# An S5/MLA encoder kernel on one core: GpSimd makes each block's powers in halves of four groups

## The chip, the cores and the metric

The kernel runs as one program on one core of a Trainium2 chip. The metric is the device time of one execution in microseconds (us). Before the change three executions took 1778.18, 1778.20 and 1778.39 us, a median of 1778.2 us.

The engines are named as the profile names them: PE is TensorE (PEld its weight loads), DVE is VectorE, ACT is ScalarE, POOL is GpSimd, and SP is SyncE, which here only issues DMAs.

## The reference, cut to what matters

Two layers over 512 positions with 1024 channels. Each layer is a half SwiGLU (1024 to 2816 and back), a mixer, and another half SwiGLU. The mixer of layer 0 is S5, a diagonal complex state-space model in 64 groups of 16 channels with 64 states; that of layer 1 is attention over a shared latent K/V.

```python
step = jnp.exp(log_step)[:, None]
lam_bar = jnp.exp(lam * step)                    # (64 groups, 64 states), complex
b_bar = ((lam_bar - 1.0) / lam)[..., None] * b
bu = einsum('gpc,bsgc->bsgp', b_bar, u)
x_t = lam_bar * x_{t-1} + bu_t                   # associative scan over 512 steps
y = einsum('gcp,bsgp->bsgc', c_re, re(x)) - einsum('gcp,bsgp->bsgc', c_im, im(x)) + d_skip * h
z = gelu(y) @ w_glu;  out = z[..., :1024] * sigmoid(z[..., 1024:])
```

The kernel takes the scan in steps of T = 8 positions. For that it needs, for each group, the powers of lam_bar up to the eighth multiplied into B and into C, and from these products small matrices (taps, and B turned) that the S5 stage uses. The change is in the making of these products.

## The kernel before, in words

The weights come as a stream of 296 packs of 128x1024 floats (N_LOADS), in order of use, into a ring of four buffers. ACT rounds each pack to its high part (split, L765), DVE subtracts to get the low part (split, L1182), and PE does three matmuls for each product of 128x128 weights with 128x512 activations: L1636, L1637 and L1638 in `three`.

The first SwiGLU is cut into two stages of 11 tiles each, FFN0A1 and FFN0A2 (HALF = 11). In the IN part of a stage PE makes a gate and an up tile for each f (48 matmuls), and DVE and ACT turn them into one tile of G: `gated` on DVE is L1192 (gate times rstd), L1194 (silu times up) and L1196 (low part of G, g_split), with ACT's L771 and L773 between them. PE starts tile f + 2 only when L1194 of tile f has read its banks (s_read). In the OUT part PE sums over the 11 tiles for each of 8 output tiles d, and DVE adds them to the residual (L1284, L1285).

The preparation of S5 runs beside these two stages, in 8 blocks of 8 groups (GB = 8, block k holds groups 8k to 8k + 7):

- POOL first makes the tables of powers (L381 to L386 in `cmul`, with 64 to 512 elements a partition), then `make_powers(k)` for each block (L564 to L600), the subject of the change. It starts the load of the next block's B and C (L581), waits for its own, and makes C times the powers in CP (L584, L589, L591, 8x9x16 = 1152 elements a partition) and B times the powers in BP (L594, L595, L597, 8x8x16 = 1024 elements). It waits on its own semaphore s_cp between a product and the subtraction that reads it. The last one raises s_made; then POOL issues the DMA that stores CP (L599). The second product into CP (L589) waits for PE's turn of the block before (s_turned) and for the store of its CP (s_cpst), because CP and BP exist once.
- Blocks 0, 1 and 2 follow each other on POOL, with more of the tables in between. Block 3 waits until the eleventh tile of G is done (L658). From block 4 on each block waits for the turn before it.
- PE turns block k in `turn_block` (L1697 to L1715): it waits for s_made, then does 16 small matmuls (L1709) and 8 transposes (L1713). Where this stands in PE's order is written out by hand in TURN_AT (L83): behind IN tiles 5, 7, 9 and OUT tile 3 of the first stage, and IN tiles 1, 3, 5, 7 of the second. PE works in order: while it waits for s_made it does nothing else.
- ACT copies the turned block out of PSUM (`copy_ops`), DVE adds the skip to the taps (`block_taps`, L1236 and L1239), and DVE makes the tables of phases (`block_tables`, L1225 to L1231: four products of 512 elements with no wait between them, a wait, then two sums). SP stores the results and needs them all before the S5 stage starts. The places in DVE's order are TAPS_AT and TABLES_AT.

```python
TURN_AT = {(FFN0A1, IN, 5): 0, (FFN0A1, IN, 7): 1, (FFN0A1, IN, 9): 2, (FFN0A1, OUT, 3): 3, (FFN0A2, IN, 1): 4,
           (FFN0A2, IN, 3): 5, (FFN0A2, IN, 5): 6, (FFN0A2, IN, 7): 7}
```

On POOL `tt` is `nc.gpsimd.tensor_tensor`. Operations of one engine are issued in order; a wait in the text is a wait of the whole engine.

Of the kernel before, what the change touches and what calls it, by code (L numbers as in the profile page):

```python
# [28 lines left out]
ALU = mybir.AluOpType  # L29
# [15 lines left out]
T = 8  # L45
STEPS = SEQ // T
GB = 8
BLOCKS = GROUPS // GB

M = T + 1  # L50
# [61 lines left out]
def build(nc, xT, wstream, cols, consts, mask, pos, lam, bcd, dskip, out):  # L112
# [40 lines left out]
    def tmp(name, shape, dt=F32):  # L153
        t = at(name, shape, dt, t_at[0])
        t_at[0] += (int(np.prod(shape[1:])) * 4 + 31) // 32 * 32
        assert t_at[0] <= o_w
        return t

    LAM = tmp("lam", [P, 3, GROUPS])
    PW = tmp("lam_pow", [P, 2, M, GROUPS])  # L160
    PWS = tmp("lam_pow_signed", [P, 2, M, GROUPS])
# [4 lines left out]
    CP = tmp("c_pow", [P, GB, M, GC])  # L166
    BP = tmp("b_pow", [P, GB, T, GC])
# [47 lines left out]
    def sem(name):  # L215
        return nc.alloc_semaphore(name)
# [31 lines left out]
    s_cp = sem("c_and_b_steps")  # L248
# [6 lines left out]
    s_made, s_turned, s_taps, s_btc = sem("powers_made"), sem("ops_turned"), sem("taps_ready"), sem("b_op_copied")  # L255
# [31 lines left out]
    def block_groups(k):  # L287

        return slice(k * GB, (k + 1) * GB)
# [132 lines left out]
    with nc.Block() as block:  # L422
# [121 lines left out]
        def _(pool):  # L544
# [8 lines left out]
            tt, ts = nc.gpsimd.tensor_tensor, nc.gpsimd.tensor_scalar  # L553
# [10 lines left out]
            def make_powers(k):  # L564

                first = k == 0

                def chan(ap):
                    return ap.rearrange("p (g c) -> p g c", g=GB)

                def power(tab, ri, n):
                    return (tab[:, ri, 0:n, block_groups(k)].rearrange("p m g -> p g m").unsqueeze(3)
                            .broadcast_to([P, GB, n, GC]))

                def spread(ap, n):
                    return chan(ap).unsqueeze(2).broadcast_to([P, GB, n, GC])

                tmc = TM[:].rearrange("p (g m c) -> p g m c", g=GB, m=M)
                tmb = TM[:, 0:GB * T * GC].rearrange("p (g m c) -> p g m c", g=GB, m=T)
                if k + 1 < BLOCKS:  # L580
                    pool.dma_start(BC[(k + 1) % 2][:], bcd[k + 1]).then_inc(s_bc[(k + 1) % 2], 16)  # L581
                bc = BC[k % 2]
                pool.wait_ge(s_bc[k % 2], 16 * (k // 2 + 1))
                tt(tmc, spread(bc[:, 3, :], M), power(PWS, 1, M), ALU.mult)  # L584
                if not first:

                    pool.wait_ge(s_turned, k)
                    pool.wait_ge(s_cpst, k * 16)
                tt(CP[:], spread(bc[:, 2, :], M), power(PWS, 0, M), ALU.mult).then_inc(s_cp, 1)  # L589
                pool.wait_ge(s_cp, k * 3 + 1)  # L590
                tt(CP[:], CP[:], tmc, ALU.subtract).then_inc(s_cp, 1)  # L591

                pool.wait_ge(s_cp, k * 3 + 2)
                tt(BP[:], spread(bc[:, 0, :], T), power(PW, 0, T), ALU.mult)  # L594
                tt(tmb, spread(bc[:, 1, :], T), power(PW, 1, T), ALU.mult).then_inc(s_cp, 1)  # L595
                pool.wait_ge(s_cp, k * 3 + 3)
                tt(BP[:], BP[:], tmb, ALU.subtract).then_inc(s_made, 1)  # L597
                pool.wait_ge(s_made, k + 1)
                pool.dma_start(ops_dram[k][:, O_C:O_T].rearrange("p (g n) -> p g n", g=GB),  # L599
                               CP[:, :, 1:M, :].rearrange("p g m c -> p g (m c)")).then_inc(s_cpst, 16)  # L600
# [41 lines left out]
            e1, e2 = (TM[:, 512 * q:512 * (q + 1)].rearrange("p (m g) -> p m g", m=T) for q in range(2))  # L642
            cmul(tt, link, PW[:, 0, 0:T, :], PW[:, 1, 0:T, :], PW[:, 0, 0:T, :], PW[:, 1, 0:T, :], ec[0], ec[1], e1, e2)
            make_powers(0)


            u1, u2, u4 = (S6[:, 5, :], S6[:, 4, :]), (S6[:, 9, :], S6[:, 10, :]), (S6[:, 11, :], S6[:, 12, :])
            squared(tt, link, u2, u1, t1, t2)
            squared(tt, link, u4, u2, t1, t2)
            squared(tt, link, (PB[:, 0, 1, :], PB[:, 1, 1, :]), u4, t1, t2)  # L650
            make_powers(1)
            powers(tt, link, PB, 7, t1, t2)
            make_powers(2)
            squared(tt, link, (PA[:, 0, 1, :], PA[:, 1, 1, :]), (PB[:, 0, 4, :], PB[:, 1, 4, :]), t1, t2)
            powers(tt, link, PA, 7, t1, t2)
# [1535 lines left out]
```

## Time and profile before

| | before |
|---|---|
| median of 3 executions | 1778.2 us |
| profiled execution | 1779.0 us |
| span of the profiled execution | 1777.2 us |
| PE busy | 1750.6 us (99%) |
| DVE busy | 933.3 us (53%) |
| ACT busy | 650.5 us (37%) |
| POOL busy | 326.4 us (18%), 276 instructions |
| mean granted clock of PE | 0.997 |

The page of the profile describes one execution; times in the trace count from the start of its span. A timeline lists an engine's instructions with their start and their duration, and in brackets the idle time before one and who ended it. A duration holds the time in which an instruction has been issued and can't run yet, so a long duration of an operation that is short elsewhere is a wait inside it. The granted clock is 1.00 for 2.4 GHz and 0.50 for 1.2 GHz. The two stages beside which S5 is prepared take the first 390 us; POOL makes blocks 0 to 2 from 50 to 122 us, and the last block ends at 281 us.

### The profile page before, as it was taken

Reading aid. Unit: us, or ns where it says so; the run is one execution under the profiler, and the core shown is the slowest. Engines: PE = TensorE matmul, PEld = TensorE weight load, DVE = VectorE, ACT = ScalarE, POOL = GpSimd, SP = SyncE. Lnnn points to the kernel's source line nnn. Section 1 sums busy time; section 2 is a strip of 40 time slices with the busy share of each in tenths; the row PEclk is TensorE's granted clock in tenths of the full one; section 3 lists DMA queues with packets and bytes.
Section 4 is the critical chain, followed back from the end, with each engine's and each line's share of the span. In section 5 each row is a group of like instructions: output and inputs, shape, how many; then the busy total and the mean of one; then the engine's idle time right before and its main releaser. Section 6 shows DMA issues by size and latency. Waiting matters only on the chain.

```text
span 1777.2 us, 22438 instructions
## 1 busy us (share of the span) xinstructions
PE 1750.6 (99%) x8598; PEld 1434.4 (81%) x8598; DVE 933.3 (53%) x1066; ACT 650.5 (37%) x896; POOL 326.4 (18%) x276
## 2 busy tenths in 40 slices
PE   9999999998999999999999999999999999999998
PEld 6888887777888888888888888888777888888887
DVE  7778888638555334433374444333774544433333
ACT  6332233347334333322253333222574443333222
POOL 8997273015013000000100000000200200000000
PEclk9999999999999999999999999999999999999999
DMA  5364555868333333333223332333310332333321
GB/s 199 121 171 131 172 158 171 294 223 269 119 95 97 98 101 94 94 95 97 94 85 111 100 94 94 95 96 101 100 36 9 121 96 94 94 95 97 101 87 48
DMA packets 80788, 206.50 MB, mean 116 GB/s; under 512 B 24048, under 2 KB 34416, under 8 KB 79696
## 3 DMA queue, kind: packets, MB, share of 16 engines
q1 hardware_dynamic: 69664, 189.86, 34.4%
q0 software_dynamic: 2592, 13.51, 2.3%
q10 hardware_dynamic: 8464, 2.20, 0.5%
q8 instruction: 47, 0.77, 0.2%
q14 instruction: 21, 0.17, 0.0%
HBM read 182.46 MB, written 23.07 MB: 116 GB/s over the span
## 4 chain that ended last, share of the span: by engine, by line
PE 89%; DVE 5%; ACT 2%; DMA 2%; issue 1%; SPq 1%; ACTq 0%; DVEq 0%
PE bank L1636 28%; PE bank L1637 28%; PE bank L1638 28%; DVE w_split L1182 1%; DMA s_y<-u_and_y 1%; PE bank L1996 1%; ACT w_split L765 1%; PE bank L1975 1%; PE bank L1809 0%; DMA x_res<-xT 0%; SPq L447 0%; DVE d_eye L1236 0%; PE bank L1988 0%; DMA y_tokens<-s_y 0%; PE bank L1713 0%
## 5 line engine op out<-in xcount | busy, mean ns | idle before, releaser
L1182 DVE TENSOR_TENSOR w_split<-w_raw,w_split 128x1024 fp32r<-128x1024 f32 x296 | 404.1, 1370 | 600.5 <-ACT w_split L765 599.6
L1636 PE MATMUL bank<-h_split,w_split 128*128 128x512 f32 x1504 | 589.8, 392 | 4.4 <-DVE gate L1194 2.7
L1638 PE MATMUL bank<-h_split,w_split 128*128 128x512 f32 x1504 | 586.0, 390 | 0.0
L1637 PE MATMUL bank<-h_split,w_split 128*128 128x512 f32 x1504 | 585.9, 390 | 0.0
L765 ACT ACTIVATE w_split<-w_raw 128x1024 fp32r<-128x1024 f32 x296 | 311.8, 1058 | 599.9 <-PE bank L1638 596.3
L1636 PEld LDWEIGHTS bank<-h_split,w_split 128*128 128x128 f32 x1504 | 282.8, 188 | 66.8 <-DVE gate L1194 3.8
L1637 PEld LDWEIGHTS bank<-h_split,w_split 128*128 128x128 f32 x1504 | 282.7, 188 | 59.4 <-issue 1.4
L1636 PE MATMUL bank<-g_split,w_split 128*128 128x512 f32 (+1 forms) x854 | 328.4, 385 | 1.9 <-DVE g_split L1196 1.5
L1638 PEld LDWEIGHTS bank<-h_split,w_split 128*128 128x128 f32 x1504 | 282.7, 188 | 58.9
L1637 PE MATMUL bank<-g_split,w_split 128*128 128x512 f32 (+1 forms) x854 | 327.6, 384 | 0.0
L1638 PE MATMUL bank<-g_split,w_split 128*128 128x512 f32 (+1 forms) x854 | 327.6, 384 | 0.0
L562 POOL TENSOR_TENSOR sq_sum<-sq_sum,sq 128x512 f32<-128x512 f32 x39 | 51.1, 1311 | 1062.5 <-ACT sq L784 953.4
L1636 PEld LDWEIGHTS bank<-g_split,w_split 128*128 128x128 f32 x854 | 160.5, 188 | 34.9 <-DVE g_split L1196 1.9
L1638 PEld LDWEIGHTS bank<-g_split,w_split 128*128 128x128 f32 x854 | 160.5, 188 | 31.8
L1637 PEld LDWEIGHTS bank<-g_split,w_split 128*128 128x128 f32 x854 | 160.5, 188 | 31.2
L771 ACT ACTIVATE gate<-gate 128x512 f32<-128x512 f32 x88 | 55.7, 632 | 232.8 <-DVE gate L1192 232.8
L1196 DVE TENSOR_TENSOR g_split<-gate,g_split 128x512 f32 (+1 forms) x88 | 77.6, 882 | 80.8 <-ACT g_split L773 80.8
L1194 DVE TENSOR_TENSOR gate<-gate,bank 128x512 f32<-128x512 f32 x88 | 60.5, 687 | 62.7 <-ACT gate L771 62.7
L773 ACT ACTIVATE g_split<-gate 128x512 f32 (+1 forms) x88 | 55.6, 632 | 72.7 <-DVE gate L1194 72.7
L1192 DVE TENSOR_TENSOR gate<-bank,rstd 128x512 f32<-128x512 f32 x88 | 60.1, 682 | 1.4 <-ACT rstd L802 1.4
L777 ACT ACTIVATE h_split<-x_res,cols 128x512 fp32r<-128x512 f32 x48 | 33.1, 717 | 52.1 <-DVE x_res L1285 48.2
L784 ACT ACTIVATE sq<-x_res 128x512 f32<-128x512 f32 x41 | 25.6, 624 | 57.3 <-DVE x_res L1285 44.9
(298 smaller groups left out, 1157.1 us busy)
## 6 DMA issues: line engine op xcount, KB each, us to landing
w_raw<-wstream SPq DMA_DIRECT2D x296, 512.0 KB, 3.5
op_slot<-s_ops SPq DMA_DIRECT2D x5, 2048.0 KB, 10.8
s_ops<-ops_out SPq DMA_DIRECT2D x16, 512.0 KB, 3.1
op_slot<-s_ops POOLq DMA_DIRECT2D x3, 2048.0 KB, 14.6
s_ops<-c_pow POOLq DMA_DIRECT2D x8, 512.0 KB, 5.4
s_ops<-k_window SPq DMA_DIRECT2D x64, 64.0 KB, 3.3
x_res<-xT SPq DMA_DIRECT2D x8, 256.0 KB, 6.5
s_u<-x_gained ACTq DMA_DIRECT2D x8, 256.0 KB, 6.1
```

The lines of the kernel that those rows point to most:

```text
L562: nc.gpsimd.tensor_tensor(ACC[:], ACC[:], SQ[:, k % 2, :], ALU.add).then_inc(s_sum, 1)
L765: nc.scalar.activation(W[:, r, 0, :], RAW[:, r, :], ACT.Copy).then_inc(s_hi, 1)
L771: nc.scalar.activation(GT[:], GT[:], ACT.Silu).then_inc(s_silu, 1)
L773: nc.scalar.activation(gt_part(f, 0), GT[:], ACT.Copy).then_inc(s_g_hi, 1)
L777: nc.scalar.activation(dst[:, k, 0, :], X[:, k, :], ACT.Identity, scale=col(gains + k)).then_inc(s_h_hi, 1)
L1182: tt(W[:, r, 1, :], RAW[:, r, :], W[:, r, 0, :].bitcast(F32), ALU.subtract).then_inc(s_lo, 1)
L1192: tt(GT[:], gb[:], RSTD[:], ALU.mult).then_inc(s_gate, 1)
L1194: tt(GT[:], GT[:], ub[:], ALU.mult).then_inc(s_read, 1)
L1196: tt(gt_part(f, 1), GT[:], gt_part(f, 0).bitcast(F32), ALU.subtract).then_inc(s_g_lo, 1)
L1636: mm(bank, hi, x_hi, start=start, stop=True, skip_group_check=True)
L1637: mm(bank, hi, x_lo, start=False, stop=True, skip_group_check=True)
L1638: return mm(bank, lo, x_hi, start=False, stop=True, skip_group_check=True)
```

## The change

Each of the six operations in `make_powers` is issued as two, one for groups 0 to 3 of the block and one for groups 4 to 7, right behind each other. The semaphore is raised by the second. The waits, the order of the six steps, the buffers and the DMAs stay as they are. A block has twelve operations in place of six, and the eight blocks 96 in place of 48.

```diff
+                def in_halves(dst, a, b, op):
+
+                    for gs in (slice(0, GB // 2), slice(GB // 2, GB)):
+                        ins = tt(dst[:, gs], a[:, gs], b[:, gs], op)
+                    return ins
+
...
-                tt(tmc, spread(bc[:, 3, :], M), power(PWS, 1, M), ALU.mult)
+                in_halves(tmc, spread(bc[:, 3, :], M), power(PWS, 1, M), ALU.mult)
                 if not first:
 
                     pool.wait_ge(s_turned, k)
                     pool.wait_ge(s_cpst, k * 16)
-                tt(CP[:], spread(bc[:, 2, :], M), power(PWS, 0, M), ALU.mult).then_inc(s_cp, 1)
+                in_halves(CP, spread(bc[:, 2, :], M), power(PWS, 0, M), ALU.mult).then_inc(s_cp, 1)
                 pool.wait_ge(s_cp, k * 3 + 1)
-                tt(CP[:], CP[:], tmc, ALU.subtract).then_inc(s_cp, 1)
+                in_halves(CP, CP, tmc, ALU.subtract).then_inc(s_cp, 1)
 
                 pool.wait_ge(s_cp, k * 3 + 2)
-                tt(BP[:], spread(bc[:, 0, :], T), power(PW, 0, T), ALU.mult)
-                tt(tmb, spread(bc[:, 1, :], T), power(PW, 1, T), ALU.mult).then_inc(s_cp, 1)
+                in_halves(BP, spread(bc[:, 0, :], T), power(PW, 0, T), ALU.mult)
+                in_halves(tmb, spread(bc[:, 1, :], T), power(PW, 1, T), ALU.mult).then_inc(s_cp, 1)
                 pool.wait_ge(s_cp, k * 3 + 3)
-                tt(BP[:], BP[:], tmb, ALU.subtract).then_inc(s_made, 1)
+                in_halves(BP, BP, tmb, ALU.subtract).then_inc(s_made, 1)
```

## Rows read from the trace of the kernel before

**Rows 1.** The page, busy time of each engine with its share of the span.
```profile
PE 1750.6 (99%) x8598; PEld 1434.4 (81%) x8598; DVE 933.3 (53%) x1066; ACT 650.5 (37%) x896; POOL 326.4 (18%) x276
```

**Rows 2.** Waits of PE, 20 to 420 us: total us, times, longest us.
```profile
PE bank L1636 <- DVE gate L1194: 2.7, 2, 1.9
```

**Rows 3.** Timeline of PE: start us, us; turns of blocks 1, 2, 6, and two waits.
```profile
99.90 0.63 PE L1709 MATMUL bank<-c_pow,b_pow 128*16 128x128 f32 x16
...
123.28 0.63 PE L1709 MATMUL bank<-c_pow,b_pow 128*16 128x128 f32 x16
...
265.74 0.63 PE L1709 MATMUL bank<-c_pow,b_pow 128*16 128x128 f32 x16
...
269.30 0.55 PE L1636 MATMUL bank<-h_split,w_split 128*128 128x512 f32 x1 [1.91 <-DVE gate L1194]
...
336.59 0.50 PE L1636 MATMUL bank<-g_split,w_split 128*128 128x512 f32 x1 [1.50 <-DVE g_split L1196]
```

**Rows 4.** Busy us of PE, PEld, DVE, ACT, POOL; granted clock, DMA share, GB/s.
```profile
269.60:273.00 3.40, 3.40 (x9) 2.65 (x8) 3.06 (x2) 2.21 (x3) 3.24 (x3) 0.50 0.51 187
...
336.00:338.00 2.00, 1.41 (x6) 1.19 (x7) 1.75 (x3) 0.76 (x1) 0.00 (x0) 1.00 1.00 412
```

**Rows 5.** DVE's weight splits, 50 to 136 us and 185 to 219 us.
```profile
L1182 DVE TENSOR_TENSOR w_split<-w_raw,w_split 128x1024 fp32r<-128x1024 f32 x16 | 34.0, 2140 | 8.3 <-ACT w_split L765 7.9
...
L1182 DVE TENSOR_TENSOR w_split<-w_raw,w_split 128x1024 fp32r<-128x1024 f32 x8 | 9.6, 1220 | 4.6 <-ACT w_split L765 4.5
```

**Rows 6.** Timeline of POOL: blocks 1, 2, 5, 6 and 7.
```profile
78.87 2.27 POOL L589 TENSOR_TENSOR c_pow<-bc_in_odd,lam_pow_signed 128x1152 f32<-128x1152 f32 x1
81.21 3.55 POOL L591 TENSOR_TENSOR c_pow<-c_pow,s_tmp 128x1152 f32<-128x1152 f32 x1
...
86.84 2.49 POOL L595 TENSOR_TENSOR s_tmp<-bc_in_odd,lam_pow 128x1024 f32<-128x1024 f32 x1
...
92.96 0.95 POOL L599 DMA_DIRECT2D s_ops<-c_pow  x1 [0.30 <-POOL b_pow L597]
...
121.84 0.95 POOL L599 DMA_DIRECT2D s_ops<-c_pow  x1 [0.30 <-POOL b_pow L597]
...
229.08 2.04 POOL L595 TENSOR_TENSOR s_tmp<-bc_in_odd,lam_pow 128x1024 f32<-128x1024 f32 x1
...
258.41 0.95 POOL L599 DMA_DIRECT2D s_ops<-c_pow  x1 [0.30 <-POOL b_pow L597]
...
269.80 2.65 POOL L591 TENSOR_TENSOR c_pow<-c_pow,s_tmp 128x1152 f32<-128x1152 f32 x1
```

**Rows 7.** Timeline of DVE beside blocks 1, 2, 5, 6 and 7.
```profile
77.78 4.45 DVE L1182 TENSOR_TENSOR w_split<-w_raw,w_split 128x1024 fp32r<-128x1024 f32 x1 [3.70 <-ACT w_split L765]
...
84.92 2.52 DVE L1196 TENSOR_TENSOR g_split<-gate,g_split 128x512 fp32r<-128x512 f32 x1 [0.70 <-ACT g_split L773]
...
93.05 1.21 DVE L1182 TENSOR_TENSOR w_split<-w_raw,w_split 128x1024 fp32r<-128x1024 f32 x1
...
121.96 0.82 DVE L1196 TENSOR_TENSOR g_split<-gate,g_split 128x512 fp32r<-128x512 f32 x1 [0.70 <-ACT g_split L773]
122.91 3.07 DVE L1182 TENSOR_TENSOR w_split<-w_raw,w_split 128x1024 fp32r<-128x1024 f32 x2
...
247.61 0.68 DVE L1192 TENSOR_TENSOR gate<-bank,rstd 128x512 f32<-128x512 f32 x1
...
258.50 1.11 DVE L1225 TENSOR_TENSOR gate<-u_pow 128x512 f32<-128x512 f32 x1
...
262.75 2.65 DVE L1230 TENSOR_TENSOR ops_out<-ops_out,gate 128x512 f32<-128x512 f32 x1
...
267.18 0.68 DVE L1192 TENSOR_TENSOR gate<-bank,rstd 128x512 f32<-128x512 f32 x1
```

**Rows 8.** Timeline of POOL: small operations of the tables, undisturbed.
```profile
26.53 0.32 POOL L386 TENSOR_TENSOR lam_pow<-lam_pow,s_tmp 128x64 f32<-128x64 f32 x1
...
33.33 0.74 POOL L385 TENSOR_TENSOR lam_pow<-lam_pow,s_tmp 128x256 f32<-128x256 f32 x1
```

## Prediction, made before the change was run

> **What bounds the kernel now.** I read the page of the profile first: TensorE (PE) is busy for 99% of the span [rows 1], so the time changes only where PE waits or loses its clock. The waits of PE up to 420 us, around the part that is changed, show two on DVE's gate operations, 2.7 us in all [rows 2]. PE's own timeline then places everything [rows 3]. The turn of block 1 begins at 99.90 and that of block 2 at 123.28: 23.38 us for 96 matmuls and a turn of 1.6 us, 0.227 us a matmul, which is PE's full pace. PE keeps it until 267.4. There it waits 1.91 us for DVE's gate (269.30); two smaller waits follow, 0.78 (the rest of the 2.7) and 1.50 us at 336.59.
>
> The first wait costs more than itself: behind it the granted clock is 0.50 (1.2 GHz, against 1.00 at 2.4 GHz) for 3.4 us, in which 9 matmuls lie where full pace has 15; half of the 3.4, 1.7 us, is lost; behind the wait of 1.50 us the clock stayed at 1.00 [rows 4]. So this part holds 1.9 + 1.7 + 0.8 + 1.5 = 5.9 us that a quicker DVE could give back, and no more.
>
> Why DVE is late there: a weight split (L1182) takes 1.22 us where POOL is idle (185 to 219), and 2.14 us on average while POOL makes powers [rows 5]. The two timelines beside each other show the cause. The split of 77.78 takes 4.45 us and ends at 82.23, right behind POOL's L589 (81.14); L591, issued at 81.21, takes 3.55 us where the one of 269.80 takes 2.65 [rows 6, 7]. A DVE operation with two SBUF inputs and a POOL operation don't run together: each waits for the whole of the other. DVE can get in between two POOL operations with no wait between them: g_split of 84.92, issued during L594, ends at 87.44, 0.6 us after the issue of L595 (86.84), and L595 takes 2.49 us for it where the one of 229.08 takes 2.04. It did not get in between L584 and L589 at 77.78, behind a DMA issue of POOL.
>
> The second thing to see is how much room POOL has. POOL issues the store of a block's powers 0.3 us after they are made: at 92.96, 121.84 and 258.41 for blocks 1, 2 and 6, whose turns begin at 99.90, 123.28 and 265.74 [rows 3, 6]. The room is 7.2, **1.7** and 7.6 us. Blocks 0 to 2 are made without a pause, so what they lose adds up in the 1.7 us.
>
> **The change part by part.** Elements, values, waits and DMAs stay; each block issues six operations more.
>
> *One more POOL operation.* With 64 elements one takes 0.32 us, with 256 elements 0.74 [rows 8]: 2.19 ns an element and 0.18 us fixed, of which 0.04 lies under the next operation. I take 0.14 us for each extra operation; the four-dimensional operands of L584 to L595 aren't shown at half size, so the bounds are 0.10 and 0.20.
>
> *Turn of block 2.* Eighteen operations more by then: 18 x 0.14 = 2.5 us (1.8 to 3.6). Then, POOL being later, DVE operations that came just behind the block fall into it and take their turns first: the g_split of 121.96 (0.6 us) and a split of 122.91 (1.1) [rows 7], 1.7 us. Last, DVE now gets in earlier, so it less often finds POOL at a DMA issue, where it costs nothing, as the split of 93.05 did beside the issue of 92.96 [rows 6, 7]; I take 0.8 us for that, between 0 and 2. Sum 2.5 + 1.7 + 0.8 = 5.0 us, less the room of 1.7: **PE waits 3.3 us** ahead of the turn of block 2 (0.1 to 5.6). PE has no slack to make it good. Everything behind it, DVE's and POOL's work paced by PE included, moves by the same amount.
>
> *Clock.* A wait of 1.91 us with a turn ahead of it was followed by 3.4 us at 1.2 GHz, a wait of 1.50 without one wasn't [rows 3, 4]. At 3.3 us with a turn behind it I count the nearer row: **1.7 us** (0 to 1.7).
>
> *DVE's chain up to 336.* From 220 to 284 POOL makes blocks 5 to 7, and DVE's chain of gates, splits, taps and tables runs behind. I stepped through it with halves of 1.2 us (L584, L589), 1.35 (L591), 1.05 (L594, L595) and 1.25 (L597), DVE taking its turn after each half. Block 5 is good for DVE: the gate of 247.61 comes 2.9 us earlier, and no more, as its split waits for PE. Block 6 isn't. DVE's tables, which now start at 258.50 just behind the block and run four in a row, start at 256 inside it, and each waits for a half; L1230, which waited 2 us of its 2.65 at 262.75, waits as long for both halves of block 7's first operation behind a DMA issue. The gate of 267.18 then comes at 267.4 [rows 7]. In block 7 POOL ends 2.7 us later than now and DVE's next tables start at 284.3, as now. Two engines that want one port all the time take as long together whatever the size of the pieces, plus 0.14 us for each extra piece. So the gain lies between 0 and the 2.9 us of block 5; small shifts decide how much of it lasts. I take half: **-1.4 us** at 336.
>
> By the Trainium skill (SBUF — State Buffer, SBUF: two separate sides) the pair of ports is locked for a whole instruction by whoever starts first. The waits for L591 agree, the split that waited through two operations doesn't; taken alone the rule makes each wait half as long, and the chain would come earlier by all that PE can use, 5.9 us.
>
> *Blocks 1, 3, 4, 6 and 7.* At nothing: the room covers them. Block 6 is the closest: the six extra operations (0.8) and the DVE operations that fall into it (about 2) leave some 5 us of 7.6, against DVE being ahead by 3. Were that gone, the turn at 265.74 would wait as that of block 2 does.
>
> **Sum.** 3.3 + 1.7 - 1.4 = +3.6 us. It is made against the profiled execution (1779.0 us, span 1777.2), which stands 0.8 us above the median of 1778.2; on the median it gives 1781.8 us.
>
> **The rivals.**
> *The shorter waits win (0.14).* Place: DVE's chain between 220 and 336. If DVE gets in at every boundary and keeps being early after block 5, it reaches 336 up to 5.9 us sooner; with 5 us of it, and POOL only 0.7 us late at the turn of block 2 (2.5 less 1.7, no clock lost), the sum is -4.3: 1773.9 us. For it: the average split loses 0.9 us beside POOL. Against: the saturated port in blocks 6 and 7. It decides from where the gate of 267.18 comes 2 us earlier.
> *Both are small (0.32).* POOL makes block 2 about 3.5 us later, PE waits 1.8 us and keeps its clock, the chain gives 1.4 back: +0.4, 1778.6 us. For it: how many DVE operations fall into block 2 is a matter of tenths.
> *The port isn't free between halves (0.12).* The change then doesn't do what it says: DVE waits for two halves as for one operation, as the split of 77.78 waited through L584 and L589. POOL is 2.5 us late or more (wait 0.8), and in blocks 5 to 7 DVE's chain is 18 x 0.14 = 2.5 us later: +3.3, 1781.5 us. Against it: the g_split of 84.92.
>
> **How the numbers follow.** The forecast has 0.42. A measurement of this kernel can tell about 0.2% from no change, 3.6 us. The forecast lies on that bound; with the spread of its own terms I put 0.29 of it above and 0.13 within. The third rival gives 0.07 and 0.05. With the second within (0.30, and 0.02 above), this makes slower 0.38, within 0.48, faster 0.14. The range: the forecast's bounds are a wait of 0.1 to 5.6, the clock's 0 to 1.7, and a gain of 0 to 2.9: from -2.8 to +7.3, with a second stretch of low clock behind a long wait a little more. Leaving 1 in 10 on either side gives 1775.5 to 1786.
>
> **What would show it.** In the profile after: L584 to L597 with 16 operations each, of 1.1 to 1.4 us where undisturbed; L599 of block 2 issued at 125 to 128 instead of 121.84; PE with a wait for POOL's b_pow ahead of L1709 at about 123.3, of some 3 us, and a clock of 0.50 behind it; L1182 in 50 to 136 at about 1.7 us instead of 2.14; the wait for the gate near 269 still there, shifted by 5. The forecast is wrong if L599 of block 2 comes before 123 (extra operations are nearly free), if that wait is below 1.5 us, or if the waits of 1.91, 0.78 and 1.50 us are gone, which would mean that DVE stays ahead once it is ahead.

## The result

| | before | after |
|---|---|---|
| median | 1778.69 us (15 executions, 1777.56 to 1780.85) | 1783.69 us (15 executions, 1779.64 to 1787.19) |
| ratio after/before | | 1.0027 (95% interval 1.0020 to 1.0033) |
| profiled execution | 1779.0 us, span 1777.2 | 1785.4 us, span 1783.6 |
| POOL busy | 326.4 us, 276 instructions | 347.8 us, 324 instructions |
| DVE busy | 933.3 us | 914.5 us |

The change makes the kernel about 4.8 us slower (0.0027 x 1778.7). The forecast was 3.6 us. The times after also spread more: 7.5 us from lowest to highest against 3.3.

The waits of PE in the kernel after, 20 to 430 us (total us, times, longest us). L1715 is L1709 of before, L1642 to L1644 are L1636 to L1638, L1200 is L1194, L1202 is L1196, L1188 is L1182, L605 is L599, and all halves are issued in L581:

```profile
PE bank L1715 <- POOL b_pow L581: 6.2, 1, 6.2
...
PE bank L1642 <- DVE gate L1200: 2.6, 3, 1.3
PE bank L1642 <- DVE g_split L1202: 1.7, 1, 1.7
```

The first line is new. The other two are four waits for DVE, 4.3 us in all; before there were three, 4.2 us in all [rows 2, and the last of rows 3]. PE's timeline says where:

```profile
99.95 0.63 PE L1715 MATMUL bank<-c_pow,b_pow 128*16 128x128 f32 x16
...
129.55 1.05 PE L1715 MATMUL bank<-c_pow,b_pow 128*16 128x128 f32 x16 [6.16 <-POOL b_pow L581]
...
274.73 0.63 PE L1715 MATMUL bank<-c_pow,b_pow 128*16 128x128 f32 x16
...
301.04 0.50 PE L1642 MATMUL bank<-h_split,w_split 128*128 128x512 f32 x1 [1.27 <-DVE gate L1200]
...
344.43 0.50 PE L1642 MATMUL bank<-g_split,w_split 128*128 128x512 f32 x1 [1.66 <-DVE g_split L1202]
```

Against [rows 3] the turn of block 2 is 6.3 us late, and that of block 6 9.0 us (274.73 less 265.74). Between the two lies a stretch of low clock, here by stretch (busy us of PE, PEld, DVE, ACT, POOL, then the granted clock):

```profile
128.60:135.20 6.60, 5.65 (x31) 4.56 (x32) 1.39 (x1) 0.03 (x1) 5.97 (x16) 0.50 0.28 91
136.00:138.00 2.00, 2.00 (x10) 1.64 (x9) 0.00 (x0) 0.00 (x0) 1.84 (x5) 1.00 0.05 8
```

PE was at full pace to 123.4, then waited, and the clock was at 1.2 GHz from before the end of the wait to 135.2. So 9.0 us is 6.2 of waiting and 2.8 of low clock. From the turn of block 6 to the wait for g_split, 344.43 less 274.73, it is 69.7 us; before it was 70.85 (336.59 less 265.74): 1.15 us are given back. The waits are not where they come from, as their sum is the same. Before, the wait of 1.91 us was followed by 3.4 us at 1.2 GHz, which cost 1.7 us [rows 4]; after, the waits are shorter pieces and the clock stays up:

```profile
136.00:344.00 208.00, 204.13 (x981) 166.63 (x979) 165.34 (x147) 67.37 (x97) 114.38 (x82) 1.00 0.55 162
```

The 1.7 us less 0.1 of longer waits would be 1.6; the 0.4 us between that and the 1.15 are not explained. Behind that the kernel after needs 1439.2 us to the end of its span, and the one before 1440.6: the one before has a stretch at 1.2 GHz near 410 us that this execution of the one after hasn't. The sum 9.0 - 1.15 - 1.4 is the 6.4 us between the two spans.

POOL's timeline shows the cause: the start of block 0, the stores that end blocks 0 to 2, and a pair of halves in block 1:

```profile
51.41 0.64 POOL L587 DMA_DIRECT2D bc_in_odd<-bcd  x1 [0.30 <-POOL lam_pow L386]
...
71.21 0.97 POOL L605 DMA_DIRECT2D s_ops<-c_pow  x1 [0.30 <-POOL b_pow L581]
...
80.53 2.40 POOL L581 TENSOR_TENSOR s_tmp<-bc_in_odd,lam_pow_signed 128x576 f32<-128x576 f32 x2
...
99.33 0.95 POOL L605 DMA_DIRECT2D s_ops<-c_pow  x1 [0.30 <-POOL b_pow L581]
...
129.80 0.95 POOL L605 DMA_DIRECT2D s_ops<-c_pow  x1 [0.30 <-POOL b_pow L581]
```

Two halves of an operation take 2.40 us where the whole takes 2.27. Block 2 is made at 129.5 instead of 121.54, 8.0 us later. Of these, 1.9 us were there at the first block already, ahead of any changed instruction: the one before started it at 49.48. The two timelines part at 33.3 us, where POOL and DVE want the port at the same moment. Before, POOL's L385, issued at 33.33, ran in 0.74 [rows 8] and DVE waited; after, it is the other way round:

```profile
33.45 1.29 POOL L385 TENSOR_TENSOR lam_pow<-lam_pow,s_tmp 128x256 f32<-128x256 f32 x1
...
33.46 0.69 DVE L1202 TENSOR_TENSOR g_split<-gate,g_split 128x512 fp32r<-128x512 f32 x1 [0.70 <-ACT g_split L779]
```

That is not the change, as the code up to there is the same in every kernel here. By the nanoseconds of the traces, POOL's L385 runs first where it is issued 9 to 24 ns ahead of DVE's g_split, and the first block starts at 49.4 to 49.8 us: in the profiles of before, e1, e2, e6, e10 and e11. Where it is 6 ns ahead or less, or up to 12 ns behind, DVE runs first and the block starts at 50.9 to 52.0: in those of after, e3, e4, e5, e7, e8 and e9. Both lists have whole blocks and halves. No kernel was profiled twice, so it isn't shown that one and the same kernel does both.

### The profile page after: what moved, and what is told of

Read it like the earlier page. It is cut to its first block, busy times and chain, and to the rows that moved or that the text cites. A ratio compares the mean times of both kernels' runs of the same rounds, so it can differ in the third digit from the quotient of the medians.

```text
span 1783.6 us, 22486 instructions
## 1 busy us (share of the span) xinstructions
PE 1749.5 (98%) x8598; PEld 1433.6 (80%) x8598; DVE 914.5 (51%) x1066; ACT 651.5 (37%) x896; POOL 347.8 (19%) x324
## 4 chain that ended last, share of the span: by engine, by line
PE 84%; POOL 6%; DVE 5%; issue 2%; ACT 2%; DMA 1%; SPq 1%; ACTq 0%; DVEq 0%; POOLq 0%
PE bank L1642 27%; PE bank L1644 27%; PE bank L1643 27%; POOL c_pow L581 1%; POOL b_pow L581 1%; POOL s_tmp L581 1%; PE bank L2002 1%; DVE w_split L1188 1%; PE bank L1981 1%; ACT w_split L771 1%; DVE state_turned L1396 0%; DMA x_res<-xT 0%; POOL s_tmp L381 0%; PE bank L1672 0%; POOL s_tmp L382 0%
## 5 line engine op out<-in xcount | busy, mean ns | idle before, releaser
L1188 DVE TENSOR_TENSOR w_split<-w_raw,w_split 128x1024 fp32r<-128x1024 f32 x296 | 400.5, 1357 | 627.6 <-ACT w_split L771 626.9
L1642 PE MATMUL bank<-h_split,w_split 128*128 128x512 f32 x1504 | 590.2, 392 | 4.7 <-DVE gate L1200 2.6
L1644 PE MATMUL bank<-h_split,w_split 128*128 128x512 f32 x1504 | 585.9, 390 | 0.0
L1642 PEld LDWEIGHTS bank<-h_split,w_split 128*128 128x128 f32 x1504 | 282.8, 188 | 67.4 <-DVE gate L1200 4.1
L1644 PEld LDWEIGHTS bank<-h_split,w_split 128*128 128x128 f32 x1504 | 282.6, 188 | 59.1
L1642 PE MATMUL bank<-g_split,w_split 128*128 128x512 f32 (+1 forms) x854 | 328.1, 384 | 1.7 <-DVE g_split L1202 1.7
L1644 PE MATMUL bank<-g_split,w_split 128*128 128x512 f32 (+1 forms) x854 | 327.6, 384 | 0.0
L1642 PEld LDWEIGHTS bank<-g_split,w_split 128*128 128x128 f32 x854 | 160.5, 188 | 33.6 <-DVE g_split L1202 2.1
L1644 PEld LDWEIGHTS bank<-g_split,w_split 128*128 128x128 f32 x854 | 160.5, 188 | 31.7
L1202 DVE TENSOR_TENSOR g_split<-gate,g_split 128x512 f32 (+1 forms) x88 | 69.8, 794 | 80.8 <-ACT g_split L779 80.8
L1200 DVE TENSOR_TENSOR gate<-gate,bank 128x512 f32<-128x512 f32 x88 | 60.5, 688 | 62.6 <-ACT gate L777 62.6
```

The lines of the kernel that those rows point to most:

```text
L1188: tt(W[:, r, 1, :], RAW[:, r, :], W[:, r, 0, :].bitcast(F32), ALU.subtract).then_inc(s_lo, 1)
L1200: tt(GT[:], GT[:], ub[:], ALU.mult).then_inc(s_read, 1)
L1202: tt(gt_part(f, 1), GT[:], gt_part(f, 0).bitcast(F32), ALU.subtract).then_inc(s_g_lo, 1)
L1642: mm(bank, hi, x_hi, start=start, stop=True, skip_group_check=True)
L1644: return mm(bank, lo, x_hi, start=False, stop=True, skip_group_check=True)
```

## The experiments

Each has 5 to 11 executions, timed beside the kernel before, whose median was 1778.3 to 1778.7 us. Times are medians, and in brackets stands the 95% interval of the ratio to the kernel before. A profile is one execution.

**e1 and e2: one part of the change alone.**

```diff
-for gs in (slice(0, GB // 2), slice(GB // 2, GB)):
+for gs in ((slice(0, GB // 2), slice(GB // 2, GB)) if k >= 3 else (slice(0, GB),)):
```

This is e1; e2 has `k < 3` in the place of `k >= 3`.

> Edit: halves in blocks 3 to 7 only; blocks 0 to 2 are made whole, as before. Theory (the loss is made in blocks 0 to 2, whose extra operations and extra turns for DVE bring POOL too late to the turn of block 2; the later halves give a little back): no wait for b_pow ahead of the turn of block 2 longer than 1 us, no stretch of 1.2 GHz behind it, and the stretch from the turn of block 6 to the first matmul of the OUT part that waits for g_split, 70.9 us before and 69.7 us with the whole change, stays at about 69.7. Time 1 us below before, ratio 0.9994 (0.998 to 1.000). Rival (the halves cost wherever they are, through the fixed price of 30 more operations, 4.2 us, on DVE's chain): ratio 1.001 or more, and that stretch is 72 us or longer.

> Edit: halves in blocks 0 to 2 only; blocks 3 to 7 are made whole. Theory: the whole loss and none of the gain. The wait ahead of the turn of block 2 is 3 to 6 us with a stretch of 1.2 GHz around it; the stretch from the turn of block 6 to the OUT wait is 70 to 71 us as before. Time 5 to 7 us above before, ratio 1.003 to 1.004. Rival (the loss isn't made there): ratio 1.000 to 1.001.

Measured: e1 0.9993 (0.9984 to 1.0002), 1776.5 us; e2 1.0049 (1.0035 to 1.0063), 1786.6 us. PE's waits, e2 first, then e1:

```profile
PE bank L1715 <- POOL b_pow L581: 3.6, 1, 3.6
```
```profile
PE bank L1642 <- DVE g_split L1202: 1.2, 1, 1.2
...
PE bank L1642 <- DVE gate L1200: 0.9, 1, 0.9
PE bank L1715 <- POOL b_pow L581: 0.9, 1, 0.9
```

The loss is made in blocks 0 to 2. It is larger in e2 than the 1.003 to 1.004 expected; the profile is of the fastest of its five executions, 1784.7 us. That execution started block 0 at 49.56, as before, and its store of block 2 is issued at 127.23: 5.4 us later than before, less the room of 1.7, gives the wait of 3.6. Its turn of block 6 is 5.3 us late, so the clock takes 1.7. In e1 the stretch from the turn of block 6 to the OUT wait is 68.1 us, 2.8 less than before and 1.6 less than expected: its waits there are 3.0 us instead of 4.2, and none is followed by a stretch of low clock (1.7 us). Its wait for b_pow is at the turn of block 7.

**e3 and e4: room at the turn of block 2.**

```diff
-            powers(tt, link, PB, 7, t1, t2)
             make_powers(2)
+            powers(tt, link, PB, 7, t1, t2)
```

> Edit on the kernel before: block 2 is made ahead of the powers of u8 (24 small operations), which don't belong to it; all operations whole. This gives POOL room at the turn of block 2. Theory: block 2 is made at 115 to 118 us instead of 121.5; where the kernel before has just enough room (1.7 us) in its profile, some of its executions are late there, so this one is 0 to 1 us faster and its times spread less: ratio 0.9995 (0.9985 to 1.000). Rival (the kernel before always has room there): ratio 1.000 with the same spread.

> Edit on the changed kernel: the same move of block 2 ahead of the powers of u8, all halves kept. Theory (the loss is only POOL's lateness at this turn): the wait for b_pow and its stretch of 1.2 GHz are gone, made at 117 to 121 us; what is left is the small gain of the later blocks. Ratio 0.9990 (0.998 to 1.000), that is 6 to 7 us below the changed kernel. Rival (the 48 extra operations or DVE's extra turns cost elsewhere too): ratio 1.001 or more.

Measured: e3 0.9999 (0.9990 to 1.0008), times 1777.5 to 1778.8; e4 0.9991 (0.9982 to 1.0000), 1776.7 us. With room the 7 us between e4 and the changed kernel are gone, with all 48 extra operations still there. e3 had the late start of block 0 (51.73) and made block 2 at 115.5. A start that is 1.9 us late costs a kernel with 1.7 us of room only 0.2 us, so its median can't tell how often the kernel before starts late; its spread, 1.3 us in 11 executions against 2.4 in 27, is too little to show it. The store of block 2 in e4, POOL's second operation of block 7, and the store of that block:

```profile
119.26 0.95 POOL L605 DMA_DIRECT2D s_ops<-c_pow  x1 [0.30 <-POOL b_pow L581]
...
269.30 3.46 POOL L581 TENSOR_TENSOR c_pow<-bc_in_odd,lam_pow_signed 128x576 f32<-128x576 f32 x2 [2.07 <-DMA s_ops<-c_pow]
...
289.29 0.93 POOL L605 DMA_DIRECT2D s_ops<-c_pow  x1 [0.30 <-POOL b_pow L581]
```

The turn of block 7 begins at 289.18 in e4, 0.2 us behind the end of the block. Before, the room was 11.7 us (made at 281.2, turn at 292.9). The 2.07 us are a wait until the store of block 6's CP has landed, as that store is issued 5.4 us later than before. Before, POOL waited there for PE's turn of block 6 alone, and its second operation of block 7 began at 267.48.

**e7: the price of eighteen instructions alone.** The kernel before, with a call of `tiny` ahead of each of the six operations, which stay whole.

```diff
+                def tiny(n):
+
+                    if k < 3:
+                        tt(STAT[:, 6 * k + n:6 * k + n + 1], PW[:, 0, 0, 0:1], PW[:, 0, 0, 0:1], ALU.mult)
...
+                tiny(0)
                 tt(tmc, spread(bc[:, 3, :], M), power(PWS, 1, M), ALU.mult)
```

> Edit on the kernel before: all operations whole, and ahead of each of the six operations of blocks 0 to 2 one POOL operation on a single element, into an unused place: 18 operations more that carry the price of issuing one and next to no work. It leaves nothing out. Theory (loss at the turn of block 2 is 2.5 us for 18 operations and about as much again for DVE's extra turns, less 1.7 us of room): each tiny operation costs 0.13 to 0.20 us, block 2 is made 2.4 to 3.6 us later, the wait for b_pow is 0.7 to 2 us, ratio 1.0005 to 1.0015, clearly less than the 1.0049 of the halves in blocks 0 to 2. Rival (the price of issuing alone makes the loss): wait of 3.5 us and ratio 1.004 or more.

Measured: 1.0024 (1.0014 to 1.0033), 1783.2 us. Two of the tiny operations and the block's store:

```profile
110.81 0.18 POOL L581 TENSOR_TENSOR attn_stat<-lam_pow 128x1 f32<-128x1 f32 x1
...
120.30 0.20 POOL L581 TENSOR_TENSOR attn_stat<-lam_pow 128x1 f32<-128x1 f32 x1
120.44 2.05 POOL L605 TENSOR_TENSOR s_tmp<-bc_in_even,lam_pow 128x1024 f32<-128x1024 f32 x1
...
126.67 0.97 POOL L610 DMA_DIRECT2D s_ops<-c_pow  x1 [0.30 <-POOL b_pow L608]
```

A tiny operation that nothing disturbs takes 0.14 to 0.15 us from its start to the next one's (120.30 to 120.44). From the start of block 0 (51.53) to the end of block 2 (126.37) it is 74.8 us, against 72.1 before (49.48 to 121.54), 77.4 in e2 and 78.1 in the kernel after. So of the 5.3 to 6.0 us that the halves cost POOL there, 2.8 are the price of eighteen more instructions and 2.5 to 3.2 what is left for the turns of DVE. Each figure is from one profile, and e7 and before didn't start alike, so the split is good to some tenths at best. The expectation of time missed: 4.3 us against at most 2.7. This profile had the late start of block 0, so its wait was 2.92 us, with a stretch of low clock behind it. Neither theory has it: eighteen more instructions with next to no work make half of e2's loss (0.0024 of 0.0049). They also make as much as the whole change (0.0027), which has the gain of the later blocks against its loss.

**e5: quarters.**

```diff
-for gs in (slice(0, GB // 2), slice(GB // 2, GB)):
+for gs in (slice(0, 2), slice(2, 4), slice(4, 6), slice(6, 8)):
```

> Edit on the kernel of e4 (block 2 ahead of the powers of u8): each of the six operations in quarters of two groups, 24 a block. Theory (DVE and POOL want one port all the time in blocks 5 to 7, so smaller pieces don't bring DVE forward; each piece costs POOL 0.14 us): another 1.7 us a block on POOL, blocks 6 and 7, which had 2.2 and 0.2 us of room before their turns in e4, are late and PE waits for b_pow there, 1 to 4 us in all. Ratio against before 1.000 to 1.003. Rival (shorter waits of DVE win): DVE's waits halve again, the waits for the gate are gone, ratio 0.998 or below.

Measured: 1.0065 (1.0051 to 1.0078), 1790.0 us. PE's waits up to 430 us:

```profile
PE bank L1715 <- POOL b_pow L581: 13.6, 3, 8.8
PE bank L1815 <- DVE state L1409: 4.4, 3, 2.1
```

The waits for the gate and for g_split are gone, all of them, and POOL is late three times, with 13.6 us: 3.1 at the turn of block 1, 1.7 at that of block 6 and 8.8 at that of block 7. The theory had the sign and was a third of the size. What the rival said of DVE is true, too. DVE's weight splits beside blocks 5 to 7 (219 to 284 us), before, after, and in quarters:

```profile
L1182 DVE TENSOR_TENSOR w_split<-w_raw,w_split 128x1024 fp32r<-128x1024 f32 x10 | 24.2, 2432 | 0.6 <-ACT w_split L765 0.5
```
```profile
L1188 DVE TENSOR_TENSOR w_split<-w_raw,w_split 128x1024 fp32r<-128x1024 f32 x11 | 20.9, 1904 | 4.7 <-ACT w_split L771 4.6
```
```profile
L1188 DVE TENSOR_TENSOR w_split<-w_raw,w_split 128x1024 fp32r<-128x1024 f32 x11 | 16.8, 1523 | 13.0 <-ACT w_split L771 12.9
```

2.43, 1.90 and 1.52 us for one: smaller pieces move the port from POOL to DVE. (In the kernel after, everything is 9 us later; e4, which isn't shifted, has 2.07 in the same window, and the kernel after has 1.93 from 228 to 293.)

**e6 and e8: fewer halves.** e6 is e4 with the first two operations of a block whole; e8 has `3 <= k <= 5` in the place of e1's `k >= 3`.

```diff
-                in_halves(tmc, spread(bc[:, 3, :], M), power(PWS, 1, M), ALU.mult)
+                tt(tmc, spread(bc[:, 3, :], M), power(PWS, 1, M), ALU.mult)
...
-                in_halves(CP, spread(bc[:, 2, :], M), power(PWS, 0, M), ALU.mult).then_inc(s_cp, 1)
+                tt(CP[:], spread(bc[:, 2, :], M), power(PWS, 0, M), ALU.mult).then_inc(s_cp, 1)
```

> Edit on the kernel of e4: the two products for C (first two operations of a block, 1152 elements) whole again, the other four in halves; 10 operations a block. Theory (behind a DMA issue DVE gets no turn between these two operations or their halves, so their halves only cost): POOL 0.28 us quicker in each block, DVE's waits as in e4; ratio 0.9985 to 0.9992, and the block 7 is made 0.5 to 1 us earlier against its turn than in e4. Rival (halves help there too): slower than e4 by 1 us or more, ratio 0.9995 or above.

> Edit: halves in blocks 3, 4 and 5 only; blocks 0 to 2, 6 and 7 whole. Theory of the prediction (block 5 in halves brings DVE's gate 2.9 us forward, and blocks 6 and 7 give it back in halves or whole): ratio 0.9990 to 1.0000; the waits for the gate behind the turn of block 6 are still there. Rival (the halves of blocks 6 and 7 are what costs the rest, by lateness of POOL): with them whole the 2.9 us stay, ratio 0.9985 or below, better than the 0.9993 of halves from block 3 on.

Measured: e6 0.9985 (0.9976 to 0.9994), 1776.3 us; e8 0.9996 (0.9987 to 1.0005), 1777.7 us. e6 is the only version whose interval lies wholly below 1: it is the fastest found, 2.7 us ahead of the kernel before. It can't be told from e4, whose interval overlaps, and the 0.5 to 1 us that it was to gain at the turn of block 7 are 0.2 (made at 288.97, turn at 289.40). The theory of e8 has its time and its wait behind the turn of block 6, which is 1.06 us instead of 1.91. That e1 is faster than e8 hints that the halves of blocks 6 and 7 help too; the intervals overlap and don't settle it.

**e9 to e11: the store of CP ahead of B's products**, with block 2 first in all; e9 has the halves of e6, e10 those from block 3 on, e11 none.

```diff
                 pool.wait_ge(s_cp, k * 3 + 2)
+                pool.dma_start(ops_dram[k][:, O_C:O_T].rearrange("p (g n) -> p g n", g=GB),
+                               CP[:, :, 1:M, :].rearrange("p g m c -> p g (m c)")).then_inc(s_cpst, 16)
...
                 pool.wait_ge(s_made, k + 1)
-                pool.dma_start(ops_dram[k][:, O_C:O_T].rearrange("p (g n) -> p g n", g=GB),
-                               CP[:, :, 1:M, :].rearrange("p g m c -> p g (m c)")).then_inc(s_cpst, 16)
```

> Edit on the kernel of e6 (block 2 first, products of C whole, the rest in halves): the DMA that stores CP is issued right behind the sum that completes CP, ahead of the products of B, instead of behind the whole block. In e6 POOL waits 2.30 us for that store before the second operation of block 7. Theory (POOL's lateness and DVE's chain share the port; POOL gets about 2 us back in block 7 and 0.3 us in each block, PE itself waits only for DVE there): the wait for the store is gone, block 7 is made 2 us earlier, PE's waits for gates and g_split change by less than 1 us in sum. Ratio 0.9975 to 0.9990, within 0.0007 of e6. Rival (POOL's end is what DVE's chain waits for, so each microsecond of POOL counts): 2 us faster than e6, ratio 0.9975 or below.

> Edit on the kernel of e9: blocks 0 to 2 whole, halves from block 3 on. Theory: halves in blocks 0 to 2 are worth nothing once block 2 has room, since PE is at full pace there: same time as e9 within 1 us, ratio 0.9975 to 0.9992. Rival (DVE being ahead in the first blocks carries on): 1 us or more slower than e9.

> Edit: block 2 first and the store of CP early as in e9, but every operation whole: what the halves themselves are worth where POOL has room. Theory (halves give DVE's chain 1 to 3 us between the turn of block 6 and the OUT part): the waits for the gate behind the turn of block 6 are 1.5 us or more again, ratio 0.9990 to 1.0000, 1.5 to 3 us slower than e9. Rival (the room is everything, the halves nothing): same as e9 within 0.5 us.

Measured: e9 0.9997 (0.9988 to 1.0006), e10 1.0001 (0.9992 to 1.0010), e11 1.0027 (1.0017 to 1.0038). The wait for the store is gone, and block 7 is made some 4 us earlier than in e6, but e9 is 1.8 us slower than e6: all its times lie above all of e6's, though the intervals overlap. Both theories of e9 missed the time. POOL and DVE in e9:

```profile
275.38 0.93 POOL L600 DMA_DIRECT2D s_ops<-c_pow  x1 [0.30 <-POOL c_pow L581]
276.33 2.18 POOL L581 TENSOR_TENSOR b_pow<-bc_in_odd,lam_pow 128x512 f32<-128x512 f32 x2
278.46 2.17 POOL L581 TENSOR_TENSOR s_tmp<-bc_in_odd,lam_pow 128x512 f32<-128x512 f32 x2
```
```profile
276.47 4.72 DVE L1202 TENSOR_TENSOR g_split<-gate,g_split 128x512 fp32r<-128x512 f32 x1 [0.70 <-ACT g_split L779]
```

The g_split, issued during the first of four halves, gets its turn behind the last, at 280.6. DVE's tables then start at 284.96 instead of 280.40, and PE gets its gate later, in one long wait:

```profile
293.81 0.71 PE L1642 MATMUL bank<-h_split,w_split 128*128 128x512 f32 x1 [2.45 <-DVE gate L1200]
```
```profile
293.90:297.30 3.40, 3.40 (x9) 2.63 (x10) 2.60 (x3) 2.41 (x3) 0.00 (x0) 0.50 0.70 268
```

The waits behind the turn of block 6 sum to 3.8 us in e6 and 3.8 in e9, as the theory had it. But those for the gate are three in e6, none above 1.1 us, and the clock stays up; in e9 they are one of 2.45 us with 3.4 us at 1.2 GHz behind it. The 1.7 us that this costs are about what e9 is slower by. e10 has the same (2.43 us, and 3.4 us at 1.2 GHz). The four halves of POOL run undisturbed: 2.18 us a pair. In e4 and e6 the same operations, with a wait and no DMA issue ahead of them, let DVE in between. e10 is within 1 us of e9, as the theory had it, so halves in blocks 0 to 2 are worth nothing that shows here; its ratio is outside the range. Whole operations in the same order (e11) are 5.6 us slower than e9, with 6.1 us of waits for the gate: there halves are worth more than the 1.5 to 3 us expected. The early store is what makes the whole operations dear: e11 differs from e3 by it alone, and e3 is 5.5 us faster.

## Why the prediction was right, and where it wasn't

The forecast was slower by 3.6 us, by POOL's lateness at the turn of block 2, with a small gain of DVE's chain against it. The time went that way (4.8 us), and e1, e2 and e4 show that the turn of block 2 is where the loss is made. The sum also had luck: the wait was longer by a late start that the prediction didn't know of, and the gain has another source than it says. Step by step:

- *Price of one more operation, 0.14 us.* Right: 2.40 less 2.27 for two halves, 0.14 to 0.15 for a tiny one.
- *Turn of block 2, wait of 3.3 us.* With the start of block 0 as in the profile of before it is 3.6 (e2). The split 2.5 + 2.5 is 2.8 + 2.5 by e7. The step didn't have what sets the start of block 0: who gets the port at 33.3 us is worth 1.9 us at the first block, and as blocks 0 to 2 run without a pause all of it arrives at the turn. In the profile after this makes 6.2 us. It may be why the times spread by 7.5 us; that isn't shown, as no run here took this race away.
- *Clock, 1.7 us.* 1.7 in e2, 2.8 behind the longer wait of the profile after.
- *DVE's chain, -1.4 us at 336.* Measured -1.15 in the profile after, -1.2 in e4, -2.8 in e1. In e2, e3 and e7, which make blocks 3 to 7 whole, the same stretch moves by -0.5, +0.2 and +0.6, so a size of 1 us is not far above what profiles differ by. The size was right, the reason wasn't: PE waits for DVE as long as before, and what is gone is the 1.7 us of low clock behind the wait of 1.91 us. "Each waits for a half" is wrong as well: the four table operations, issued back to back, kept the port, and POOL's pair waited for all of them. DVE and POOL after, in block 6:

```profile
263.87 1.12 DVE L1231 TENSOR_TENSOR gate<-u_pow 128x512 f32<-128x512 f32 x1
264.92 1.12 DVE L1232 TENSOR_TENSOR up<-u_pow 128x512 f32<-128x512 f32 x1
265.97 1.10 DVE L1233 TENSOR_TENSOR ops_out<-u_pow 128x512 f32<-128x512 f32 x1
267.00 1.11 DVE L1234 TENSOR_TENSOR ops_out<-u_pow 128x512 f32<-128x512 f32 x1
```
```profile
262.65 6.45 POOL L581 TENSOR_TENSOR s_tmp<-bc_in_even,lam_pow 128x512 f32<-128x512 f32 x2
```

The same row of four beside block 4 did take turns with POOL's halves:

```profile
178.22 2.05 DVE L1231 TENSOR_TENSOR gate<-u_pow 128x512 f32<-128x512 f32 x1
180.20 2.35 DVE L1232 TENSOR_TENSOR up<-u_pow 128x512 f32<-128x512 f32 x1
```

In the traces the row kept the port where its first operation got it at once (1.1 us) and POOL was already waiting, and took turns where its first operation had to wait (2.05 us here). Why, no run here settles. PE no longer waits behind the turn of block 6, and waits of 1.3, 0.4 and 0.9 us come behind block 7's instead. "Two engines that want one port all the time take as long together whatever the size of the pieces" holds for the two together only: e5 shows that smaller pieces let DVE be early at POOL's cost.

- *Blocks 1, 3, 4, 6 and 7 at nothing.* Right for PE in the kernel after, and by luck: the room of block 6 is 2.2 us (made at 272.5, turn at 274.73) where some 5 were forecast, that of block 7 is 0.2 (made at 297.91, turn at 298.11), and of the 7.2 us of block 1 0.9 is left (made at 99.03, turn at 99.95). The step left out that a later store of CP makes POOL wait for it (2.1 us).
- *The splits of 50 to 136 us at about 1.7 us.* Wrong: 2.15 on average, as before. At least one reason is that DVE's waits behind a DMA issue last through four halves as through two whole operations; in the kernel after this one lasts through both pairs from 52.06 to 56.8:

```profile
51.58 6.34 DVE L1188 TENSOR_TENSOR w_split<-w_raw,w_split 128x1024 fp32r<-128x1024 f32 x1
```

- *Rival "the shorter waits win".* Its place and its cap were real; e6, which has the halves without the turn of block 2, gets 2.7 us of the 5.9, of which 1.7 is the clock's by its profile. By the Trainium skill (SBUF — State Buffer, SBUF: two separate sides) the lock is held for one instruction. The traces agree between most neighbours (the halves and the row at 178.22 to 186.8 take turns), and differ behind a DMA issue of POOL (4.72 us in e9) and in the rows of four beside blocks 6 and 7 (6.45 us), where the lock went on to the next instruction of the same engine.
- *Rival "the port isn't free between halves".* True behind a DMA issue only, and there nearly always.

## What to carry to other kernels

Cutting the operations of a side engine smaller moves a shared port from it to the other engine; it costs a fixed price for each piece plus the turns that the other one now takes. Add both up to every point at which the bounding engine waits for the side engine, and carry them over blocks that follow without a pause. Look there for room first: moving unrelated small work behind the block that is due left 8.1 us of room in e3 (made at 115.5, turn at 123.7) where it was 1.7, at no cost in time. With that room (e4, e6), or with blocks 0 to 2 left whole (e1), the halves no longer cost; a gain that is clear of noise is shown for e6 alone, 0.9985. And look at how waits are cut up, not only at their sum: one wait of 2.45 us with low clock behind it cost 1.7 us more than three that sum to the same.

## What the runs showed of the hardware

- POOL and DVE take turns at the port between neighbouring operations, but not always. Behind a DMA issue of POOL a waiting DVE operation mostly got no turn until POOL's next wait: 4.72 us through four halves in e9, 4.45 us through two whole operations before [rows 6, 7]. There are exceptions: in e9 at 252.4 us, where POOL's first half had itself waited for DVE (1.28 us instead of 1.12), DVE got its turn behind it.
- DVE can keep it in the same way: four operations of 1.1 us in a row made POOL's pair take 6.45 us instead of 2.18. Beside block 4 the same four took turns with POOL's halves.
- Two requests for the port within 24 ns of each other: in six profiles POOL, 9 ns ahead or more, went first, in seven DVE did. It was worth 1.9 us at the next block.
- A wait of PE of 2.45 us was followed by 3.4 us at 1.2 GHz, three waits of 1.05 us and less in the same stretch by none (e9 and e6). Waits of 1.9 us fell on both sides: one of 1.91 before had 3.4 us at 1.2 GHz behind it, one of 1.93 in e7 at 274.05 had none.
- A POOL operation on one element cost 0.14 to 0.15 us from its start to the next one's, where nothing disturbed it (e7).
